# mLSTM last head: the order of the four new-state blocks among the products, their PSUM banks and their copies

## The reference, cut to what matters

```python
def _mlstm_chunk(carry, inp):
    C, n, m = carry
    q, k, v, li, lf = inp
    ...
    s = jnp.einsum('bhtd,bhsd->bhts', q, k) * jnp.exp(dmat - m_t[..., None])
    num = w_inter[..., None] * jnp.einsum('bhtd,bhde->bhte', q, C) + jnp.einsum('bhts,bhse->bhte', s, v)
    nq = w_inter * jnp.einsum('bhtd,bhd->bht', q, n) + jnp.sum(s, axis=-1)
    h = num / jnp.maximum(jnp.abs(nq), jnp.exp(-m_t))[..., None]
    ...
    C_new = g_state[..., None, None] * C + jnp.einsum('bhs,bhsd,bhse->bhde', g_tok, k, v)
    n_new = g_state[..., None] * n + jnp.einsum('bhs,bhsd->bhd', g_tok, k)

# the mixer, after the heads
hn = _layernorm_heads(hs, g_head...)
out = (hn + skip * xc) * jax.nn.sigmoid(z)
return out @ w_down, (C, n, m, ...)
```

## Time and profile before

| | us |
|---|---|
| three runs, median | 1812.82 (1811.86 to 1814.65) |
| the profiled execution, device time | 1810.58 |
| its span on the core | 1808.6 |
| PE busy | 1765.2 (98%) |
| DVE busy | 1142.0 (63%) |
| ACT busy | 875.7 (48%) |

### The profile page before, as it was taken

The page is one execution under the profiler, slowest core; times in us unless marked ns, Lnnn a source line. Parts: engine busy times, 40 slices in busy tenths (PEclk is TensorE's granted clock), DMA queues, the critical chain, the costliest instruction groups (busy, mean ns, idle before and its releaser), DMA issues.

```text
span 1808.6 us, 33987 instructions
## 1 busy us (share of the span) xinstructions
PE 1765.2 (98%) x13177; PEld 1643.0 (91%) x13177; DVE 1142.0 (63%) x1856; ACT 875.7 (48%) x1470; POOL 160.4 (9%) x111
## 2 busy tenths in 40 slices
PE   7999999999999999999999999999999999999997
PEld 6999855999999979999997799999999964999997
DVE  5886577565556546664576676555887568666543
ACT  4565422455444385554454555544565422455443
POOL 0000132110011002000120020011000034110000
PEclk9999999999999999999999999999999999999999
DMA  4555334555555614555543155555455424555552
GB/s 150 175 159 172 100 117 163 191 163 165 168 164 171 188 61 153 163 164 165 168 118 114 48 163 164 167 169 164 146 164 175 146 83 160 190 163 163 164 168 90
DMA packets 155883, 272.94 MB, mean 151 GB/s; under 512 B 22693, under 2 KB 28274, under 8 KB 155770
## 3 DMA queue, kind: packets, MB, share of 16 engines
q1 hardware_dynamic: 155770, 271.37, 48.3%
HBM read 250.55 MB, written 20.78 MB: 150 GB/s over the span
## 4 chain that ended last, share of the span: by engine, by line
PE 88%; DVE 7%; ACT 3%; DMA 1%; issue 1%; SPq 0%; ACTq 0%; DVEq 0%
PE PS L1773 86%; PE PS L1778 2%; ACT PB L949 1%; DVE C L1325 1%; DVE WLO L1056 1%; DVE QT L1360 0%; DVE NB L1316 0%; DMA out_p_C_dram<-CPST 0%; DMA RAWT<-in_c_w_ukv_dram 0%; DMA XIN<-in_x_sample_dram 0%; DVE TMP L1635 0%; DVE QT L1365 0%; DVE BST L1302 0%; DVE KS L1292 0%; DVE HL L1371 0%
## 5 line engine op out<-in xcount | busy, mean ns | idle before, releaser
L1056 DVE TENSOR_TENSOR WLO<-RAWT,WHI 128x512 fp32r<-128x512 f32 (+1 forms) x904 | 636.5, 721 | 490.1 <-ACT WHI L651 488.0
L651 ACT ACTIVATE WHI<-RAWT 128x512 fp32r<-128x512 f32 (+1 forms) x904 | 554.8, 626 | 653.4 <-PE PS L1773 650.8
L1773 PE MATMUL PS<-XGH,WHI 128*128 128x288 f32 x1776 | 527.3, 297 | 7.1 <-DVE WLO L1056 7.0
L1773 PE MATMUL PS<-HH,WLO 128*128 128x288 f32 (+1 forms) x1792 | 529.7, 296 | 0.0
L1773 PE MATMUL PS<-HH,WHI 128*128 128x288 f32 (+1 forms) x1792 | 528.9, 295 | 0.4 <-issue 0.4
L1773 PE MATMUL PS<-HL,WHI 128*128 128x288 f32 (+1 forms) x1792 | 528.6, 295 | 0.0
L1773 PE MATMUL PS<-XGH,WLO 128*128 128x288 f32 x1776 | 525.5, 296 | 0.0
L1773 PE MATMUL PS<-XGL,WHI 128*128 128x288 f32 x1776 | 524.6, 295 | 0.0
L1773 PEld LDWEIGHTS PS<-XGH,WHI 128*128 128x128 f32 x1776 | 333.7, 188 | 11.1 <-DVE WLO L1056 8.0
L1773 PEld LDWEIGHTS PS<-HH,WHI 128*128 128x128 f32 x1792 | 336.6, 188 | 3.7 <-issue 3.6
L1773 PEld LDWEIGHTS PS<-HH,WLO 128*128 128x128 f32 x1792 | 336.7, 188 | 0.0
(11 more groups left out here) (364 smaller groups left out, 1410.2 us busy)
## 6 DMA issues: line engine op xcount, KB each, us to landing
RAWT<-in_w_ff_dram SPq DMA_DIRECT2D x256, 512.0 KB, 3.8
RAWT<-in_a_w_up_dram SPq DMA_DIRECT2D x64, 512.0 KB, 3.8
RAWT<-in_a_w_down_dram SPq DMA_DIRECT2D x32, 512.0 KB, 3.7
RAWT<-in_b_w_qkv_dram SPq DMA_DIRECT2D x24, 512.0 KB, 3.8
RAWT<-in_a_w_q_dram SPq DMA_DIRECT2D x16, 512.0 KB, 3.8
RAWT<-in_a_w_k_dram SPq DMA_DIRECT2D x16, 512.0 KB, 3.7
RAWT<-in_a_w_v_dram SPq DMA_DIRECT2D x16, 512.0 KB, 3.8
C<-in_state_mlstm_C_dram SPq DMA_DIRECT2D x8, 1024.0 KB, 5.9
```

The source lines that it names most:

```text
L651: act.activation(hi, raw, ACT.Copy).then_inc(weight_hi, 1)
L1056: dve.tensor_tensor(lo, raw, hi, ALU.subtract).then_inc(weight_lo, 1)
L1773: return pe.matmul(out, lhsT, rhs, start=start, stop=stop, **kw)
```

## The change

In the last head of each mLSTM layer, and only there, it changes four things. The banks of the new-state blocks become 6, 6, 3, 2 instead of 6, 3, 2, 6. On PE `new_state(1)` moves from behind `sample(3)` to directly behind the QT x C0 products, ahead of the one-column products, and waits for the copy of block 0; `new_state(2)` stands where `new_state(1)` stood; `new_state(3)` stands where `new_state(2)` stood, ahead of the transposes of NSB, and nothing stands any more between these and the transpose of NOUT. On ACT the copy of block 0 is ahead of the head's `rsqrt`, and the copy of block 1 is then the only one before the sample's `rsqrt`. `last_state(0)` waits for two copies (a wait for three stands just before it and stays), and the wait for all four copies goes behind `old_state(3, 0)`, ahead of the first unit of the down projection. SP's stream is not changed.

```diff
--- before.py
+++ after.py
@@ -356,7 +356,7 @@
             return (4, 5, 6, 7, 4, 5, 0, 2, 0, 2, 0, 2)[x]
 
         def new_bank(h, b):
-            return 3 - b % 2 if h < AH - 1 else (6, 3, 2, 6)[b]
+            return 3 - b % 2 if h < AH - 1 else (6, 6, 3, 2)[b]
 
         def gain(nu):
 
@@ -806,6 +806,8 @@
                 act.wait_ge(cvs_dma, 32 * (la + 1))
                 for h in range(AH):
                     U = AH * la + h
+                    if h == AH - 1:
+                        state(4 * U)
                     rsqrt(U, 2, hvar_out, hy_out)
                     if h + 1 < AH:
                         decay(h + 1)
@@ -813,11 +815,14 @@
                     act.wait_ge(ecol_out, la + 1)
                     act.activation(QCP[:, 0:512], PS[:, 2 if h + 1 < AH else 1, :], ACT.Copy,
                                    scale=AECOL[:, 12 + h:13 + h]).then_inc(qcp_out, 1)
-                    for b in range(4):
-                        if h == AH - 1 and b == 2:
-                            rsqrt(la, 1, svar_out, sy_out)
-                        state(4 * U + b)
-                    if h == AH - 1:
+                    if h < AH - 1:
+                        for b in range(4):
+                            state(4 * U + b)
+                    else:
+                        state(4 * U + 1)
+                        rsqrt(la, 1, svar_out, sy_out)
+                        state(4 * U + 2)
+                        state(4 * U + 3)
                         act.wait_ge(nst_done, la + 1)
                         act.activation(NST[:], PS[0:32, 0, 0:P], ACT.Copy).then_inc(nst_out, 1)
                         act.wait_ge(smo_out, la + 1)
@@ -2042,6 +2047,9 @@
                     for b in range(4):
                         ins = mm(PS[32 * b:32 * b + 32, 1 if last else 2, :], QT[:, 4 * h + b, TP:T], C0[:, h % 2, b, :])
                     ins.then_inc(qc_done, 1)
+                    if last:
+                        pe.wait_ge(cp_out, 4 * U + 1)
+                        new_state(1)
 
                     def columns():
                         pe.wait_ge(kg_out, 2 * U + 2)
@@ -2078,23 +2086,21 @@
                     mm(PS[32 * j:32 * j + 32, 7, 3:4], I4[:], QCP[:, 512 + j:513 + j])
                 sample(h).then_inc(ns_done, 1)
                 pe.wait_ge(cs_out, 2 * U)
-                new_state(1)
+                new_state(2)
                 pe.wait_ge(nqs_out, la + 1)
                 columns()
                 turn()
-                new_state(2)
+                new_state(3)
                 pe.wait_ge(sn_out, la + 1)
                 for a in range(4):
                     ins = xp(PS[:, 1, a * P:(a + 1) * P], NSB[:, a * P:(a + 1) * P])
                 ins.then_inc(sxp_done, 1)
-                pe.wait_ge(cp_out, 4 * U + 1)
-                new_state(3)
                 pe.wait_ge(n_out, U + 1)
                 xp(PS[0:32, 0, 0:P], NOUT[:].rearrange("p s f -> p (s f)")).then_inc(nst_done, 1)
 
                 def last_state(b0):
                     if b0 == 0:
-                        pe.wait_ge(cp_out, 4 * U + 4)
+                        pe.wait_ge(cp_out, 4 * U + 2)
                     else:
                         pe.wait_ge(hg_out, U + 1)
                     old_state(AH - 1, b0)
@@ -2418,6 +2424,7 @@
                     def ready(k):
                         if k == 0:
                             last_state(0)
+                            pe.wait_ge(cp_out, 4 * AH * (la + 1))
                             pe.wait_ge(nst_out, la + 1)
                             pe.wait_ge(smh_lo, la + 1)
                         if k == 2:
```

## The result

| | before | changed |
|---|---|---|
| median of the runs timed together | 1813.23 us (8 runs, 1811.74 to 1814.65) | 1817.93 us (8 runs, 1816.24 to 1822.59) |
| ratio, 95% interval | | 1.0029 (1.0021 to 1.0038) |
| the profiled execution, span | 1808.6 us | 1817.2 us |
| its mean granted clock of TensorE | 0.998 | 0.993 |

The change makes the kernel slower by 0.29%, about 5 us. The forecast was +1.14 us, 1814.0 us, with 1816.2 as the upper end; the measured median lies above that end. The page of the changed kernel looks almost like that of before: PE is busy for 9.5 us more and the last slice of the clock is lower.

A forecast was written before the change was run, and what follows sets the result against it. PE, busy 98% of the span, was taken as the bound, with the down projection's start deciding per layer. Layer 3's +0.94 and layer 0's +0.20 gave +1.14 us on the 1812.82 us median: 1814.0 us, range 1811.8 to 1816.2.

The forecast's parts named there:

- What bounds the kernel, and the start of the down projection as the number that decides: PE is busy 98% of the span and gapless from the down projection on, so its start decides in each layer.
- `new_state(1)` in the gap for QCP, +1.14 us: Ahead of sample(3): a 1.9 us block put into a 0.76 us gap makes new_state(2) start 1.14 us after new_state(1)'s old start.
- The transposes of NSB 1.14 later, and the gap: Last head, layer 3: transposes move from 1533.03 to 1534.17; a 2.4 us PE gap opens ahead of the down projection.
- Layer 3 +0.94, layer 0 +0.20: Later start of the down projection in us; layer 0 wins back 0.74 us of waiting for a store.
- The two hand-overs: Waits between engines in the sample's chain ahead of the down projection, one of them 0.03 us to ACT's high part.
- No wait for a copy in layer 0: Layer 0 ahead of the down projection: the store is hidden, as ACT finishes NST at 303.77, before the sample's QT at 303.94.
- rival 3: A store holds ACT's copies longer ahead of the down projection: slower, bounded near +1.2 us, 1815.2 us; chance 0.05.
- Rival 4, the clock: PE's clock falls to half behind the new 2.4 us gap ahead of the down projection: slower than 0.2%; chance 0.03.
- The price of rival 4, 6.7 us: Down projection's first two units at half speed in both layers: 6.7 us more, 1820.7 us; chance 0.03.
- The baseline: Profiled execution of 1810.58 us, 2.24 under the three-run median of 1812.82 us, on which the sum was put.

The follow-up runs named there:

- e3: The changed kernel with new_state(3) moved back behind the four transposes of NSB; ratio to the kernel before 1.0001.
- e8: The kernel before with only the early ACT copy of block 0, ahead of the last head's square root; ratio 0.9997.
- e12: The kernel before with block 3 in bank 3, and on ACT NST, then the sample's high part, ahead of block 3's copy; ratio 1.0001.
- e1: The kernel before, unchanged, measured once more; ratio 0.9995.
- e9: The changed kernel, unchanged, measured once more; ratio to the kernel before 1.0026.
- e4: The kernel before with ACT doing the sample's high part five times in a row, making a 2.86 us gap ahead of the down projection; ratio 1.0046.
- e10: The changed kernel with two unused products filling PE's gap ahead of the down projection in layer 0 only; ratio to the kernel before 1.0010.
- e7: The kernel before with ACT doing the sample's high part three times in a row, making a 1.54 us gap ahead of the down projection; ratio 1.0038.
- e2: The changed kernel with two unused products on PE behind old_state(3, 0) in both layers; ratio to the kernel before 1.0002.

## Why the prediction was wrong, point by point

- *What bounds the kernel, and the start of the down projection as the number that decides*: right. PE runs without a gap behind it, and the starts moved by what the chain of the sample moved by.
- *`new_state(1)` in the gap for QCP, +1.14 us*: right in its cause and size. `new_state(1)` starts at 1531.27, 0.08 before the end of the group ahead of it (0.07), 1.92 to the next group (1.90), `new_state(2)` at 1534.24, 2.89 from zero (2.91).
- *The transposes of NSB 1.14 later, and the gap*: right, 8.38 - 7.25 = 1.13, and 2.61 us for 2.4. The working had NSB done 0.54 us ahead of the transposes (1533.63 against 1534.17), so that without PE's block they could start that much earlier at most. e3 confirms this link: taking the block away won 0.60 us, though my expectation for e3 had 1.0 to 1.2.
- *Layer 3 +0.94, layer 0 +0.20*: measured 1.07 and 0.33, in sum 1.40 for 1.14. The two hand-overs that I took at 0.03 us and 0.10 took 0.04 and 0.22 (low part to PE); that is most of it.
- *No wait for a copy in layer 0*: wrong, and without cost. `old_state(3, 0)` waited 1.1 to 1.4 us in all five profiles with this order, since block 2's copy started 9.5 to 9.9 us from zero where it had been 8.4. The store of block 1 now follows that of block 0 closely, which speaks for rival 3's mechanism, but the same landing was as late in e8 and e12, where it doesn't. It stayed hidden behind the sample's chain.
- *Rival 4, the clock*: this is the step that failed. The sum had no term for the clock behind the new gap, and the rival that had one got a chance of 0.03. The mechanism was named, with its place, and it is what happened: 1.5 us in each layer of the first profile. I put it aside because a gap of 2.58 us at 34.03 "shows no dent". In e1 the same gap in the same program is followed by windows at 0.50, and it was low there in 11 of the 15 profiles. One execution without a fall had told me only that the clock *can* survive such a gap. The reading of the page was too coarse as well: its slices are 45 us long, and the changed kernel's page shows nines at 309 and 1545 us, where the clock was halved for 3.4 us.
- *The price of rival 4, 6.7 us*: too high. It let both first units of each layer, 24 products, run at half speed from end to end; they took 1.5 us longer in each layer, 3.1 us in all, and not in every execution. Over all 16 runs of the changed kernel the mean clock is 0.9934, over 102 of before 0.9951. At the full 1.8 us for 0.001 the difference is 3.1 us, at the fitted 1.2 us it is 2.0. With the 1.4 us of order that is 3.4 to 4.5 us; the mean times of the same runs differ by 1817.76 - 1813.18 = 4.58 us. So the sum that should have stood there is +1.4 for the order and +2 to +3 for the clock, and up to 1.2 us stays without an account.
- *The baseline*: I took the profile of before for a typical run. It was 2.2 us under the median, and I put that down to spread. Its mean clock of 0.998 said what it was: the 102 runs of before have 0.990 to 0.998, and the 18 at 0.997 and 0.998 took 1811.1 us in the mean, 2.1 us less than all. With a typical profile the clock would have shown as a cost that comes and goes.

What stays open: the low stretch near 1456 us, at the start of layer 3's mix, 70 us ahead of the changed instructions of that layer. It is there in five of the six profiles with a longer gap in either layer (not in e9), and in none of the nine others. No run here says how a gap in layer 0 would reach it, or whether it is chance. Open too is what decides in one execution whether the clock falls behind a gap: its length alone doesn't.

## What to carry to other kernels

When a change closes small gaps on TensorE and leaves one large one, add up the time at half clock behind it, and not only the idle time: here the order cost 1.4 us and the clock 2 to 3. Before trusting "the clock is at full speed throughout", look at the mean granted clock of many runs and at windows of a few us behind each gap, since one execution and 45 us slices hide it. And a block of work fills a wait for nothing only if it is no longer than the wait: 1.9 us put into 0.76 us moved everything behind it that was on the critical chain.

## What the runs showed of the hardware

- The granted clock fell to half behind gaps of idle PE, and whether it did varied between executions of the same program: at the 2.58 us gap near 34 us it held in the first profile of before and fell in e1, and at layer 0's 1.27 + 1.27 us it held in e9 and fell in the profile of the changed kernel (1.09 + 1.46 us). Behind gaps of 2.6 to 2.9 us in layer 3 it fell in all four profiles (changed, e4, e9, e10), and behind 1.54 us in e7. Behind layer 3 gaps of up to 1.07 us it fell in none of ten. In layer 0 it fell behind 1.04 us in e3 and held behind 1.15 us in e12, so the length of one gap doesn't settle it. By the rule of the Trainium skill ("TensorE: Matmul & The Clock Gate", "HAM oscillation — how this bites in real kernels") an idle PE is sent back to half clock, and the traces agree with that; the page's example waits 3 to 5 us for a DMA each time, and here 2.6 us and less were enough. The same page ("What's actually happening") says that the monitor behind this runs free of the kernel, so that the moment at which the clock changes varies from run to run. e1 and e9 fit that; no run here shows the monitor itself.
- A low stretch right behind the start of the down projection cost 1.53 us: from the first product to the group of `last_state(2)` took 3.34 us without one and 4.87 with one, in both layers and in every profile except the layer 0 of e2 and e10 (3.67 us, the unused products run into it) and of e4 and e7 (5.9 and 6.0 us, the clock was low about twice as long).
- The record of the granted clock doesn't show the start of the kernel. In the first profile of before it says 1.00 from the first instruction on, but the first products of the first projection start 0.24 us apart, as at half clock, until about 19.5 us; from there on it is 0.13 us.

```profile
16.00:20.00 4.00, 3.77 (x17) 3.80 (x18) 3.57 (x6) 1.99 (x6) 0.00 (x0) 1.00 0.43 130
...
17.09 0.44 PE L1773 MATMUL PS<-XGH,WHI 128*128 128x288 f32 x1
17.33 0.44 PE L1773 MATMUL PS<-XGL,WHI 128*128 128x288 f32 x1
```

- Unused products, 1.7 us of them in each of the two gaps (1.5 and 2.6 us directly ahead of the down projection), brought a whole kernel of 1818 us down by 0.27% (e2).
- The spread between runs of the kernel before goes with the mean clock of each run: the 18 at 0.997 and 0.998 took 1810.2 to 1812.7 us, the 32 at 0.995 1812.0 to 1815.4, and the 11 at 0.993 and less 1815.1 to 1820.2 us.
